# Three norms summed by GpSimd adds and one matmul, in place of grouped 32-column matmuls

## The reference

```
def rms_norm(x, g):
    xf = x.astype(jnp.float32)
    y = xf * lax.rsqrt(jnp.mean(xf * xf, axis=-1, keepdims=True) + EPS)
    return (y * g.astype(jnp.float32)).astype(x.dtype)

h  = rms_norm(x,  norm_pre[l]) * (1.0 + sc[:, None])  + sh[:, None]     # the stream
hc = rms_norm(xc, norm_pre[l]) * (1.0 + scc) + shc                      # the context
z  = h @ w_in[l];  zc = hc @ ...
...                                            # attention, long convolution, gMLP, merge
x_new = x + gt[:, None] * rms_norm(out, norm_post[l])                   # and the same for xc
```

## Time and profile before

| | |
|---|---|
| median of three runs | 1902.87 us (1902.48 to 1903.45) |
| the profiled execution: span on the page | 1899.9 us |
| the profiled execution: own time of the run | not given apart; the median is 3.0 us above the span |
| TensorE matmul, weight load | 99% and 84% busy |
| VectorE, ScalarE, GpSimd | 70%, 53% and 2% busy |
| granted TensorE clock | 0.9 or more of full speed in each of the 40 slices |

### The profile page before, as it was taken

How to read it: one execution, slowest core, us unless ns; L and a number is a source line. 1 busy time by engine, 2 the same in 40 slices (tenths; PEclk the granted TensorE clock), 3 DMA queues, 4 the chain that set the end, 5 groups by cost and what they waited for, 6 DMA issues and landing times.

```text
span 1899.9 us, 26256 instructions
## 1 busy us (share of the span) xinstructions
PE 1874.5 (99%) x10688; PEld 1587.0 (84%) x10688; DVE 1337.0 (70%) x1826; ACT 1004.9 (53%) x1462; POOL 39.0 (2%) x47
## 2 busy tenths in 40 slices
PE   7999999999999999999999999999999999999998
PEld 3899888999888998988788887788888888778887
DVE  5788789888789878855755566755566555786555
ACT  3465544564544655444544456554455444666444
POOL 1300000000000000000000000000000000000000
PEclk9999999999999999999999999999999999999999
DMA  9645675535676644465567754367755776536775
GB/s 364 223 147 182 222 241 195 188 124 174 221 246 198 211 156 134 155 220 187 161 219 225 225 190 144 133 210 220 228 197 181 226 226 213 182 111 197 226 230 166
DMA packets 123319, 375.17 MB, mean 197 GB/s; under 512 B 14080, under 2 KB 32640, under 8 KB 122432
## 3 DMA queue, kind: packets, MB, share of 16 engines
q1 hardware_dynamic: 118320, 352.11, 56.0%
q0 software_dynamic: 4592, 19.90, 3.0%
q10 hardware_dynamic: 288, 1.51, 0.2%
HBM read 360.87 MB, written 10.49 MB: 195 GB/s over the span
## 4 chain that ended last, share of the span: by engine, by line
PE 92%; DVE 5%; ACT 1%; DMA 1%; issue 1%; SPq 0%; DVEq 0%; ACTq 0%
PE PS L676 28%; PE PS L678 27%; PE PS L677 27%; DVE w_lo L2110 2%; PE PS L850 1%; PE PS L869 1%; DMA raw<-weights 1%; PE PS L1258 1%; ACT w_hi L1512 1%; PE PS L1091 1%; PE PS L959 1%; PE PS L1247 1%; PE PS L940 1%; PE PS L859 0%; PE PS L813 0%
## 5 line engine op out<-in xcount | busy, mean ns | idle before, releaser
L2110 DVE TENSOR_TENSOR w_lo<-raw,w_hi 128x1024 fp32r<-128x1024 f32 x600 | 731.7, 1233 | 390.9 <-ACT w_hi L1512 389.4
L1512 ACT ACTIVATE w_hi<-raw 128x1024 fp32r<-128x1024 f32 x600 | 625.3, 1057 | 446.9 <-DMA raw<-weights 443.9
L676 PE MATMUL PS<-w_hi,h_hi 128*128 128x512 f32 (+1 forms) x1280 | 494.9, 387 | 2.1 <-DVE w_lo L2110 1.3
L678 PE MATMUL PS<-w_hi,h_lo 128*128 128x512 f32 (+1 forms) x1280 | 488.4, 382 | 0.0
L677 PE MATMUL PS<-w_lo,h_hi 128*128 128x512 f32 (+1 forms) x1280 | 488.1, 381 | 0.0
L676 PEld LDWEIGHTS PS<-w_hi,h_hi 128*128 128x128 f32 x1280 | 240.7, 188 | 54.8 <-issue 5.1
L678 PEld LDWEIGHTS PS<-w_hi,h_lo 128*128 128x128 f32 x1280 | 240.7, 188 | 47.2
L677 PEld LDWEIGHTS PS<-w_lo,h_hi 128*128 128x128 f32 x1280 | 240.9, 188 | 45.5 <-issue 1.0
L676 PE MATMUL PS<-h_hi,w_hi 128*128 128x256 f32 x896 | 258.3, 288 | 0.7 <-issue 0.3
L676 PE MATMUL PS<-w_hi,g_hi 128*128 128x512 f32 (+1 forms) x656 | 257.1, 392 | 0.1
L677 PE MATMUL PS<-h_lo,w_hi 128*128 128x256 f32 x896 | 253.4, 283 | 0.0
(11 more groups left out here) (302 smaller groups left out, 1663.8 us busy)
## 6 DMA issues: line engine op xcount, KB each, us to landing
raw<-weights SPq DMA_DIRECT2D x610, 512.0 KB, 3.9
act_mem<-arena SPq DMA_DIRECT2D x144, 64.0 KB, 3.0
arena<-act_mem SPq DMA_DIRECT2D x36, 256.0 KB, 3.6
qk<-weights POOLq DMA_DIRECT2D x12, 512.0 KB, 4.2
v<-weights POOLq DMA_DIRECT2D x12, 512.0 KB, 5.1
x<-weights SPq DMA_DIRECT2D x8, 512.0 KB, 8.0
qk<-cond_in POOLq DMA_DIRECT2D x2, 1024.0 KB, 5.1
arena<-arena SPq DMA_DIRECT2D x32, 64.0 KB, 2.6
```

Source lines behind the costliest of these rows:

```text
L676: pe.matmul(dst, hi, m_hi_, start=first, stop=False, **kw)
L678: return pe.matmul(dst, lo, m_hi_, start=False, stop=last, **kw)
L1512: nc.scalar.activation(w_hi[:, r, :], raw[:, r, :], ACT.Copy).then_inc(w_hi_ready, 1)
L2110: V.tensor_tensor(w_lo[:, r, :], raw[:, r, :], f32(w_hi[:, r, :]), ALU.subtract).then_inc(w_lo_ready, 1)
```

## The change

For norms 2, 1 and 4 GpSimd adds the pieces of squares, two slices at a time, into the first (`add_squares`, three adds of 128x512), and then the two slices left into one (`sum_squares`, one add of 128x256). TensorE multiplies that one slice by all 128 columns of `ones` (`norm_summed`). The grouped matmuls, ScalarE's copy and the matmul with `share` stay for norms 0, 3 and 5 only. For norms 2 and 4 `norm_summed` stands where the groups stood, right behind the last merge group; for norm 1 where the total stood. On GpSimd the adds stand in the queue of the modulation's loads: those of norms 2 and 4 behind the sixth, eighth and tenth load of the pass and the last one behind the twelfth, those of norm 1 behind all of pass 0's loads. The two semaphores of the gate row become one.

```
+            def add_squares(nid, c):
+                pool.wait_ge(sq_ready, 4 * MS_ORDER.index(nid) + c + 1)
+                if c > 1:
+                    pool.wait_ge(sq_added, adds[0])
+                s = sq_behind[:, 0:2, :]
+                nc.gpsimd.tensor_tensor(s, s, sq_behind[:, 2 * c:2 * c + 2, :], ALU.add).then_inc(sq_added, 1)
+                adds[0] += 1
+            def sum_squares():
+                pool.wait_ge(sq_added, adds[0])
+                nc.gpsimd.tensor_tensor(sq_behind[:, 0, :], sq_behind[:, 0, :], sq_behind[:, 1, :], ALU.add).then_inc(sq_summed, 1)
...
                 for n in range(first + 2, end):
                     pool.wait_ge(ada_sum, 2 * (n - 1))
                     load_ada(n)
+                    if n - first in (5, 7, 9):
+                        add_squares([2, 4][p], (n - first - 3) // 2)
+                sum_squares()
             modulation_rows(0)
+            for c in range(1, 4):
+                add_squares(1, c)
+            sum_squares()
             modulation_rows(1)
...
+            def norm_summed(nid):
                 if nid in (2, 4):
                     pe.wait_ge(sel_ready, 3 * nid)
+                pe.wait_ge(sq_summed, SUMMED.index(nid) + 1)
+                pe.matmul(PS[:, NORM_BANK(nid), 0:T], ones[:, :], sq_behind[:, 0, :], start=True, stop=True).then_inc(ms_ready, 1)
...
-                    if j == 1 and behind_second is not None:
-                        norm_groups(behind_second)
                     if j == 2 and behind_second is not None:
-                        norm_total(behind_second)
+                        norm_summed(behind_second)
...
             run_pass(0)
-            norm_groups(2)
-            branch_sum(0, 0)
-            norm_total(2)
-            for j in range(1, 4):
+            norm_summed(2)
+            for j in range(4):
                 branch_sum(0, j)
...
-                if behind_second is not None:
-                    copy_groups(behind_second)
...
-                if p < 2:
-                    copy_groups([2, 4][p])
...
+SUMMED = [2, 1, 4]
+GROUPED = [0, 3, 5]
```

More of the change, by code:

```diff
@@ L381, in build @@
         sq_ready = sem("sq_ready")
+        sq_added = sem("sq_added")
+        sq_summed = sem("sq_summed")
         ms_groups = sem("ms_groups")
@@ L429, in build @@
         tail_loaded = sem("tail_loaded")
-        gate_stored = sem("gate_stored")
-        gate_loaded = sem("gate_loaded")
+        gate_moved = sem("gate_moved")
         out_done = sem("out_done")
@@ L645, in load_ada @@
                 pool.dma_start(ada_w[n % 2], weights[dram_pass[1] - ADA_SLOTS + n]).then_inc(ada_w_loaded[n % 2], 16)
+            adds = [0]
+            def add_squares(nid, c):
[8 more added lines that the diff above has]
+                nc.gpsimd.tensor_tensor(sq_behind[:, 0, :], sq_behind[:, 0, :], sq_behind[:, 1, :], ALU.add).then_inc(sq_summed, 1)
             def modulation_rows(p):
@@ L664, in _ @@
             pool.wait_ge(gated_ready, 18)
[L665 to L668, removed]
+            pool.dma_start(gate_mem.rearrange("o (p k) -> p (o k)", p=P), gate_cols).then_inc(gate_moved, 16)
+            pool.wait_ge(gate_moved, 16)
+            pool.dma_start(gate_row, gate_mem.to_broadcast([P, D])).then_inc(gate_moved, 16)
+            pool.wait_ge(gate_moved, 32)
             pool.dma_start(layer[:, 0:ntail], tail_in).then_inc(tail_loaded, 16)
@@ L733, in token_pair, with norm_groups @@
                     mm.then_inc(w_used, 1)
-            def norm_groups(nid):
+            def norm_summed(nid):
                 if nid in (2, 4):
                     pe.wait_ge(sel_ready, 3 * nid)
+                pe.wait_ge(sq_summed, SUMMED.index(nid) + 1)
+                pe.matmul(PS[:, NORM_BANK(nid), 0:T], ones[:, :], sq_behind[:, 0, :], start=True, stop=True).then_inc(ms_ready, 1)
+            def norm_groups(nid):
                 for kk in range(KD):
@@ L746, in norm_total @@
             def norm_total(nid):
-                pe.wait_ge(ms_copied, MS_ORDER.index(nid) + 1)
+                pe.wait_ge(ms_copied, GROUPED.index(nid) + 1)
                 pe.matmul(PS[:, NORM_BANK(nid), 0:T], share[:, :], rt, start=True, stop=True).then_inc(ms_ready, 1)
@@ L1461, in _ @@
             run_pass(1)
[L1462 to L1465, removed]
+            norm_summed(4)
+            for j in range(4):
                 branch_sum(1, j)
@@ L1530, in copy_groups @@
             def copy_groups(nid):
-                act.wait_ge(ms_groups, MS_ORDER.index(nid) + 1)
+                act.wait_ge(ms_groups, GROUPED.index(nid) + 1)
                 nc.scalar.activation(rt, PS[:, NORM_BANK(nid), 0:T], ACT.Copy).then_inc(ms_copied, 1)
@@ L2563, in last_sums @@
                 splits(c, 6)
-                dve.wait_ge(gate_loaded, 16)
+                dve.wait_ge(gate_moved, 32)
                 scale_out(0)
```

## The result

The median rose from 1903.45 us (1902.44 to 1908.11, 9 runs) to 1909.74 us (1906.61 to 1914.58, 9 runs): ratio 1.0031, 95% interval 1.0023 to 1.0040. I had forecast 1901.8, and the range ended at 1904.9.

What follows compares the result with a forecast made beforehand. TensorE, busy for 99% of the span, was taken as the bound. Removing 3.1 us from it and adding 2.0 us of VectorE held by GpSimd gave -1.1, from 1902.87 to 1901.8 us; eight-in-ten range 1899.6 to 1904.9.

Steps and rivals of the forecast that it cites:

- The gain: TensorE at the three norms: 1.00 us each at norms 2 and 4 and 1.1 at norm 1, 3.1 removed.
- The bounds of the gain: TensorE's removed work at the three norms was to lie between 2.6 and 3.3 us.
- The gain of norm 1: Behind the second pair of pass 1: removing the groups takes 1.1 us off TensorE, between readings of 1.00 and 1.19.
- The cost of the first and second add: In the merge groups: each add delays VectorE's next merge add and TensorE by 0.5 us, bounds 0 to 1.2.
- rival (b): At four places before TensorE's `w_lo` waits VectorE loses a whole add, 1.2 us each: 1904.6, or 1905.8 with half adds; 20%.
- The half adds: Last add of norms 2 and 4: through before the next merge add starts, cost 0, bound 0.6 us.
- The third add: Three `w_lo` start 0.95 us late, but TensorE waits for none and VectorE idles behind them: cost 0.
- The sums come in time: GpSimd's sums are ready before TensorE asks: margin over 12 us at norms 2 and 4, 2.3 at norm 1; cost zero.
- The sum: Over the whole span: -3.1 us removed plus 2.0 us added gives -1.1 us, so 1901.8 us.
- The range: For eight in ten, the time was to lie from 1899.6 to 1904.9 us.

Runs made afterwards that it cites:

- adds_moved: Changed kernel with the adds of norms 2 and 4 moved behind the seventh and ninth loads of the pass: 1900.98 us, 0.9988 of the kernel before.
- norm1_only: Kernel before with norm 1 alone summed by GpSimd, norms 2 and 4 left grouped: 1902.82 us, 0.9997 of the kernel before.
- later_half: Changed kernel with a 128x512 GpSimd fill in front of each add of norms 2 and 4: 1905.28 us, 1.0008 of the kernel before.
- later_little: Changed kernel with a 128x64 GpSimd fill in front of each add of norms 2 and 4: one run, 1904.5 us against 1903.69.
- later_tiny: Changed kernel with a 128x1 GpSimd fill in front of each add of norms 2 and 4: one run, 1904.2 us against 1903.28.
- narrow_all: Changed kernel with GpSimd's new adds cut to 16 columns of each tile, so sums are wrong: 1900.84 us, 0.9982 of the kernel before.
- moved_early: adds_moved with norm 1's squares on ScalarE two and two behind the weight splits, hence earlier: 1902.21 us, 0.9992 of the kernel before.
- moved_grouped: adds_moved with norm 1 back in grouped 32-column matmuls and three copies: 1902.28 us, 0.9991 of the kernel before.

## Why the prediction was wrong, step by step

**The gain** was sized rightly where it arises. Norms 2 and 4 gave 0.95 each (forecast 1.00), norm 1 gave 1.18 (forecast 1.1), which is the 1.19 that the prediction had read between starts, and not the chain's 1.00. The bounds of the gain were added up wrongly: the text's own terms give 2.5 to 3.2 and not 2.6 to 3.3, and nothing hangs on it.

**The gain of norm 1 doesn't last.** The step "I take 1.1" asked what the groups hold, and not what comes next on TensorE's way. Some 20 us on, TensorE needs VectorE's mix. From slot 88 to 100 the changed kernel keeps 0.25 us of the 1.18 (2.19 to 1.94), adds_moved 0.11.

The slack of 0.36 us in the trace of before is not what sets this, since VectorE had its pause of 0.62 there and could have come earlier as well. What sets it shows in the ten traces of the changed kernel and its variants. In all ten kernels VectorE works without a pause of over 0.05 us from the `w_lo` of slot 96 to the end of the mix, in 19.79 to 19.81 us (20.50 with the pause in the kernel before). So the mix comes when that `w_lo` starts, plus 19.8. The `w_lo` needs the load of slot 96, and this load is issued when slot 91 ends, 345.22 in the kernel before, that is where norm 1's groups begin (345.12 to 346.12) and not behind them. What TensorE gains at norm 1 comes too late to bring it forward.

Two things differ from kernel to kernel: how long the load took, and how late VectorE came to the `w_lo` after `w_hi` was ready. The last column is an estimate, 0.93 less what both are above those of the kernel before; the 0.93 is fitted to the eight rows, and it is what would be kept at the load and lateness of the kernel before (us):

```
kernel          load   VectorE late   kept of 1.18   estimate
before          3.76       0.03            -             -
after           4.00       0.46          0.25          0.25
norm1_only      3.50       0.97          0.25          0.24
later_half      3.75       0.71          0.27          0.26
later_little    4.48       0.03          0.21          0.20
later_tiny      4.89       0.03         -0.20         -0.22
narrow_all      4.34       0.03          0.33          0.34
moved_early     4.68       0.03          0.00         -0.01
adds_moved      4.58       0.03          0.11          0.10
```

So, by this estimate, 0.25 of the 1.18 is lost in any case, and two things add to the wait at the softmax. One is a load that took longer than in the kernel before, by up to 1.1 us; why it did is open. The other is norm 1's adds: where VectorE was late at this `w_lo`, it was still behind from the two earlier ones that the adds had held up. In the changed kernel the 0.93 are 0.25, 0.24 from the load and 0.43 from the adds. In norm1_only, whose load was the shortest, there would have been no wait without the adds. The chain of the changed kernel has one of the two `w_lo` in it:

```profile
347.03 2.31 DVE w_lo L2128
349.34 1.15 DVE arena L2280
```

The lead of norm 2 is there before slot 91, so it does bring the load forward: in moved_grouped the load is issued 1.01 earlier and takes 1.07 longer, the pause of 0.62 is used up, the mix ends 0.63 earlier, and with the slack of 0.36 TensorE loses only 0.14 (-1.00 to -0.87).

**The cost of the first and second add** is the step that failed. It said that the running merge add would be finished first and the next one delayed by what is left of the add, 0.5. Measured were 1.38, 1.36, 1.37 and 1.39: one whole add (1.30) and 0.08 more, because the running instruction, not the next, stood still. That is the price of rival (b), for which I had 20%, and a little more than the bound "1.2, a whole add" of the forecast; but not by the route that (b) named: the add was not 0.7 us later and the product was not held. The evidence that I leaned on was a `w_lo` that started beside a running add in the earlier trace rows. It shows that an instruction that is clearly second waits; it doesn't show who is first when both start within a few tenths. later_half, later_little and later_tiny gave the 0.63 and 0.38 that belong to the case I had assumed.

The Trainium skill (SBUF — State Buffer, section "SBUF: two separate sides") says that of two such instructions on VectorE and GpSimd, whichever starts first gets the pair of SBUF ports that they share for the whole instruction. By the recorded starts the traces disagree at close range: directly behind a load's issue, leads of VectorE from 0.20 to 0.36 us lost against a full add; with no issue directly ahead, leads from 0.30 on kept. That one of the two runs undisturbed to its end and the other waits, the traces bear out in every case.

**The half adds** were put at nothing with a bound of 0.6. They took 0.82 and 0.83, the half add's 0.75 and again 0.08 more. Here too the merge add running at 295.56 lost to an add that began 0.22 later.

**The third add** was right at zero: three `w_lo` took 4.41 in place of 3.49 and TensorE didn't wait.

```profile
278.96 4.41 DVE L2128 TENSOR_TENSOR w_lo<-raw,w_hi 128x1024 fp32r<-128x1024 f32 x3
```

**The sums come in time**, as predicted; TensorE waits for GpSimd nowhere. Norm 1's adds took 1.66 each and two `w_lo` 4.12 in place of 2.36. The prediction wrote that TensorE waits for no `w_lo` between 340 and 360 us, and that held; but VectorE was still 0.46 late from it at the `w_lo` of slot 96, and that reached TensorE at the softmax, as said above.

```profile
343.28 4.99 POOL L656 TENSOR_TENSOR arena<-arena 128x512 f32<-128x512 f32 x3 [46.75 <-ACT arena L1545]
348.34 1.60 POOL L662 TENSOR_TENSOR arena<-arena 128x256 f32<-128x256 f32 x1
```
```profile
345.23 4.12 DVE L2128 TENSOR_TENSOR w_lo<-raw,w_hi 128x1024 fp32r<-128x1024 f32 x2 [2.95 <-ACT w_hi L1534]
```

**The sum** by the measured terms: forecast -3.1 + 2.0. Measured -3.1 at the norms, +5.5 and +1.65 at the merge groups, +0.9 at the softmax, +0.37 at the end of pass 1, which is 5.4, and drifts of -0.4 take it to 4.99. Of the miss of 6.1 us (-1.1 against 4.99) 5.15 are in the adds (7.15 measured, 2.0 forecast). The medians differ by 6.3 us, the profiled spans by 4.9; the rest is spread of the runs of the changed kernel (1906.61 to 1914.58), of which the profiled one was the fastest.

**The range** ended at 1904.9, though the text had worked out 1905.8 for all adds lost at once. I had treated the six places as if some would be lost and some not; but they share one phase (load, add, merge add), so that they fall together, and the 20% of (b) belonged to its full price. Even that price is short of the result. What it lacked were the 0.2 us by which each place cost more than the 1.2 or 0.6 taken for it, the 0.9 at the softmax and the 0.37 at the end of pass 1, of which none had a bound in the text.

## What to carry to other kernels

An add on GpSimd can cost VectorE its whole length when it begins beside an instruction with two SBUF inputs, even if VectorE began a little earlier (up to 0.36 us here, behind a load's issue); so price such a place at the whole instruction, and look for a place where TensorE isn't waiting for VectorE's next results. Moving the adds by one load turned +5 us into -1.6 and made the best version of this study. Where one phase repeats, its places win or lose together, and the range must hold both. And a gain on TensorE counts only as far as the next place where TensorE meets a dense stretch of another engine lets it through: look for the first such place downstream, follow the other engine back to what started its stretch, and ask whether the gain comes before or after that. Here it was a load issued just ahead of the gain.

## What the runs showed of the hardware

- GpSimd's add of 128x512 against an instruction of VectorE with two SBUF inputs. Directly behind a DMA issue of GpSimd, VectorE's lead of 0.20 (merge add 2.07 in place of 0.69), 0.32 (`w_lo` 2.72 in place of 1.22) and 0.36 us (2.75) was not enough, nor was 0.22 against the half add (1.52); 0.92 us was. With no issue directly ahead, 0.30, 0.34, 0.38 and 0.45 us were enough. Against an add of 2x16 columns directly behind an issue, 0.21 us was enough. So neither the lead nor the issue nor the size decides alone, and the rule behind it stays open.
- The loser waits to the winner's end: a merge add then ended 0.56 us after the add, a `w_lo` 1.09 us after it.
- A fill by GpSimd (128x512 in 0.55 us), which reads nothing, ran beside a merge add of VectorE without harm to either.
- A product of one PSUM and one SBUF input on VectorE ran its 0.68 us beside GpSimd's add.
- Groups of 32-column matmuls: taking sixteen records away from a stream of projections brought the next matmul 1.09 us forward and the one behind it 1.19.
- The load of one slot of weights (512 KB), issued at the same point of the program, took 3.50 to 4.89 us in eleven profiled executions.
